# Cross attention's scores in three one-pass fp32r products instead of one fp32 product

## The chip, the core and the metric

The kernel runs on one core of a Trainium2 chip. The metric is the device time of one execution in microseconds; lower is better. The kernel before takes 1884.87 us, the median of 3 runs (1883.82 to 1886.38). The chip's engines run beside each other, each through its own list in order, and wait for each other by semaphores: TensorE (PE, with its weight loads shown as PEld), VectorE (DVE), ScalarE (ACT), GpSimd (POOL) and SyncE (SP), which here issues most DMAs.

## The reference

Two layers of a decoder trunk on 512 tokens of width 1024, batch 1, all in float32. Each layer is a mixer (forgetting attention and a gated recurrence in layer 0, a spatial gating mixer in layer 1), then cross attention into 256 memory tokens, then a mixture of 32 experts. The change is in cross attention, which both layers have:

```python
def memory_cross_attention(xn, memn, wq, wkv, wo, q_gain, k_gain):
    B, S, _ = xn.shape
    q = rms_norm((xn @ wq).reshape(B, S, X_HEADS, X_HEAD_DIM), q_gain)
    k, v = jnp.split(memn @ wkv, 2, axis=-1)
    k = rms_norm(k.reshape(B, MEM_LEN, X_HEADS, X_HEAD_DIM), k_gain)
    v = v.reshape(B, MEM_LEN, X_HEADS, X_HEAD_DIM)
    s = jnp.einsum('bqhd,bkhd->bhqk', q, k, preferred_element_type=jnp.float32) * X_HEAD_DIM ** -0.5
    p = jax.nn.softmax(s, axis=-1).astype(v.dtype)
    o = jnp.einsum('bhqk,bkhd->bqhd', p, v).reshape(B, S, D_MODEL)
    return o @ wo
```

There are 4 heads of 256 channels, so a head's channels fill two blocks of 128 partitions; the whole width is eight blocks, j = 0 to 7, and head h has blocks 2h and 2h + 1.

## The kernel before

Everything is written out by hand: each engine has its own program, and the order of its instructions is the order of the code. Numbers in brackets after L are lines of the kernel.

The large projections are done in float32 by splitting. ScalarE rounds a weight tile of 128 x 512 to fp32r (wh, L575), VectorE computes what is left over (wl, L589 with the norm's gain, L586 without), and TensorE adds three one-pass products: high by high, low by high, high by low (L718, in the helper `dense`). One weight tile is a step. The buffers hold three steps, so a step's wl must be there before TensorE begins the step, and can't be written earlier than three steps ahead. Other work is woven between steps: a `between` table gives for a step's number what an engine does before that step.

Cross attention of a layer runs so:

1. The memory's projection to keys and most of the values (kv 0 to 2), then the queries' projection (xq 0 and 1). Between steps 4 and 6 of xq 0 TensorE turns the normalised keys (L1032); VectorE copies them out of PSUM with their gain to xkT (`k_out`, L2214).
2. The last part of the values' projection (kv 3). Between its steps TensorE turns the first four blocks of the normalised queries xqn (`turn`, L1048), ScalarE copies them with their gain to xqT (`turned`, L1648, signal q_out), and VectorE sums squares and scales the second half of xqn (L1912).
3. The softmax loop over 16 items; an item n is a head and 128 queries. For each n, TensorE does the scores of item n + 3 (`scores`, L1058), turns the probabilities of item n (`transposes`, L1067), after items 1, 3, 5, 7 the next query block (`turn` 4 to 7), and after items 4, 8, 12 the value products of a whole head (`values`, L1077). VectorE takes the maximum of a row of scores (L2230), and per item a reciprocal and the scaling of the probabilities (L2235, L2236); ScalarE does the exponential (L1667), the copy of the turned probabilities (L1675), xqT (L1648) and the high part of a head's output (L1681), whose low part is VectorE's `output_lo` (L2241).
4. The output projection (xo), then the routing and the experts.

Scores need a query block in xqT and the keys in xkT; three PSUM banks hold scores, so item n's scores wait until the exponential of item n - 3 has read its bank (p_done). Query blocks are turned in two PSUM banks, 2 and 3, so `turn(j)` waits until block j - 2 has been copied out.

SyncE issues the loads of the weights in one fixed order. Twelve buffers take expert weights; six are the ring that dense weights use too, others lie over tiles that the earlier stages use, slot7 over `nat` (memory tokens) and slot8 over `gain`. `free_slot` holds what a load waits for.

Of the kernel before, what the change touches and what calls it, by code (L numbers as in the profile page):

```python
# [18 lines left out]
F32 = mybir.dt.float32  # L19
# [7 lines left out]
P = 128  # L27
# [183 lines left out]
def program(nc, A, out):  # L211
    ctx = ExitStack()
    with ctx:
# [73 lines left out]
        def sm(name):  # L287
# [65 lines left out]
        xkn = sb("xkn", [P, MM, D], over="extra", skip=24 * E)  # L353
        xkT = sb("xkT", [P, KD, MEM], over="extra", skip=32 * E)
        xv = sb("xv", [P, MM, D], over="extra", skip=40 * E)
        xqT = sb("xqT", [P, KD, T], over="extra", skip=48 * E)
        xqn = sb("xqn", [P, TM, D], over="extra", skip=16 * E)
# [74 lines left out]
            "rg_sqrt rec_ready rec_hi rec_lo gate_ready "  # L432
            "rows_clear c_rows fs_done fe_done fo_done fo_copied fo_ready fo_hi fo_lo q_turned q_out s_done mx_done p_done pn_done pt_done pt_copied o_done o_hi o_copied "
            "gains_loaded gains_loaded2 gains_turned gains_ready f_scaled k_rounded k_copied gb_scaled u_scaled u_out blocks_loaded mem_loaded spatial_done v_pre v_out vbias_loaded bs_loaded v_scaled ws_loaded ws_masked ws_turned wsT_ready gt_ready gt_hi gt_lo "
# [186 lines left out]
        def _(sp):  # L621
            def free_slot(unit, l):
# [10 lines left out]
                elif SLOT[unit] == RING + 1:  # L633
                    sp.wait_ge(acc_done, PLAIN["nmem", l, MM - 1] + 1)
                    sp.wait_ge(squares, nats_upto("mem", l))
                elif SLOT[unit] == RING + 2:
                    sp.wait_ge(S["rec_ready"], 4)
                elif SLOT[unit] == RING + 3:
                    sp.wait_ge(S["pt_done"], N_ITEMS * (l + 1))
                elif SLOT[unit] == RING + 4:  # L640
                    sp.wait_ge(S["o_done"], X_HEADS * (l + 1))
                elif SLOT[unit] in (RING + 5, ONCE):
                    sp.wait_ge(acc_done, PLAIN["route", l, 0] + 1)
# [50 lines left out]
        def _(pe):  # L694
# [324 lines left out]
            def cross(l):  # L1019
# [22 lines left out]
                def turn(j):  # L1042

                    pe.wait_ge(heads_ready, n0 + 3 + j // 4)
                    if j >= 2:
                        pe.wait_ge(S["q_out"], q0 + (j - 1 if j < 4 else j))
                    for m in range(TM):
# [3 lines left out]
                def scores(n):  # L1051
                    h, i = items_x[n]
                    if i == 0:
                        pe.wait_ge(S["q_out"], q0 + max(2 * h + 2, 4))
                    if n >= SCORES:
                        pe.wait_ge(S["p_done"], t0 + n - SCORES + 1)
                    for kk in range(2):
                        mm = pe.matmul(ps[:, SCORE_BANK[n % SCORES], 0:MEM], xqT[:, 2 * h + kk, i * P:(i + 1) * P],  # L1058
                                       xkT[:, 2 * h + kk, :], start=(kk == 0), stop=(kk == 1))
                    mm.then_inc(S["s_done"], 1)  # L1060
# [789 lines left out]
        def _(dve):  # L1850
# [346 lines left out]
            def cross(l):  # L2197
# [12 lines left out]
                def k_out(r):  # L2210
                    def run():
                        b = round_done(dve, ("xkT", l, r))
                        for j in range(4):
                            ins = dve.tensor_scalar(xkT[:, 4 * r + j, :], ps[:, b + j, 0:MEM], xkg[:, l, j % 2:j % 2 + 1],  # L2214
                                                    None, ALU.mult)
                        ins.then_inc(took(("xkT", l, r)), 1)
                    return run
# [5 lines left out]
                means = lambda *ms: lambda: head_means(("xq", l, 1), ms, 2, X_DIM)  # L2223
                split(("kv", l), 3, {3: means(0, 1), 4: means(2, 3), 7: xqh(1)})
                split_next()
                t0, h0 = N_ITEMS * l, X_HEADS * l

# [22 lines left out]
                for n in range(N_ITEMS):  # L2250
                    normalise(n)
                    if n + SCORES < N_ITEMS:
                        maxima(n + SCORES)
                    if n % TM >= 2 and n > TM:
                        output_lo(n // TM - 1, n % TM - 2)
# [496 lines left out]
```

## Time and profile before

| | |
|---|---|
| median of 3 runs | 1884.87 us |
| profiled execution | 1886.64 us, span 1884.9 us |
| mean granted TensorE clock | 0.996 |
| PE busy | 1848.6 us, 98% |
| DVE busy | 860.6 us, 46% |
| ACT busy | 558.2 us, 30% |
| scores of cross attention (L1058), PE | 32.9 us busy, 128 records of 128x256 |

The span is the time from the first to the last instruction of one profiled execution. A matmul's record is longer than the time it holds TensorE, since the next one starts before it ends: what matters in a row of equal matmuls is the distance between starts. An fp32 product shows as two records, an fp32r product as one; an fp32 turn shows as one. Rows that read "x4" join four neighbouring records of the same form. TensorE's records write f32 for both.

### The profile page before, as it was taken

The page shows a single profiled execution, that of the slowest core. Times are in us where ns is not written, and L with a number is a line of the kernel's source. Part 1 is how long each engine was busy: PE and PEld are TensorE (multiplying, and loading weights), DVE is VectorE, ACT ScalarE, POOL GpSimd, SP SyncE. Part 2 cuts the span into 40 slices and gives each one's busy share as a digit, 9 for nine tenths or more (in the row PEclk, how much of TensorE's full clock was granted, in tenths as well). Part 3 has the DMA queues.
Part 4 walks back from the last instruction along what each step waited for, and adds up shares of the span by engine and source line. Part 5 has one row for each costly group of instructions (what it writes and reads, how often), then busy time and mean ns, then how long its engine had stood idle before and what let it go on. Part 6 is the DMA issues. An engine that isn't in the chain of part 4 may idle for free.

```text
span 1884.9 us, 22147 instructions
## 1 busy us (share of the span) xinstructions
PE 1848.6 (98%) x9054; PEld 1168.7 (62%) x9054; DVE 860.6 (46%) x1384; ACT 558.2 (30%) x1015; POOL 101.1 (5%) x144
## 2 busy tenths in 40 slices
PE   8999999999999999999899999999999999999997
PEld 7775778686454444543588888787784444544543
DVE  4566564546342433433433455455363433433433
ACT  4436353633111111111344433445351111111110
POOL 2200010001000000000000022000010000000000
PEclk9999999999999999999999999999999999999999
DMA  6220243137999999999633321332159999999997
GB/s 238 90 67 23 90 139 107 46 104 306 399 421 421 421 421 420 421 421 421 231 125 116 106 88 69 112 134 90 49 201 370 421 421 422 421 420 421 421 421 298
DMA packets 95640, 486.92 MB, mean 258 GB/s; under 512 B 7776, under 2 KB 7888, under 8 KB 46256
## 3 DMA queue, kind: packets, MB, share of 16 engines
q1 hardware_dynamic: 93408, 479.23, 63.8%
q0 software_dynamic: 1456, 5.14, 0.9%
q8 instruction: 76, 1.25, 0.3%
q10 hardware_dynamic: 672, 1.07, 0.2%
q14 instruction: 28, 0.23, 0.0%
HBM read 483.31 MB, written 2.10 MB: 258 GB/s over the span
## 4 chain that ended last, share of the span: by engine, by line
PE 92%; DMA 3%; DVE 3%; ACT 2%; issue 0%; POOL 0%; SPq 0%; DVEq 0%; POOLq 0%; ACTq 0%
PE ps L718 27%; PE ps L1161 22%; PE ps L1185 11%; PE ps L715 7%; PE ps L1126 6%; PE ps L1147 5%; PE ps L1077 1%; DMA slot<-in_moe_w_down 1%; DMA ring<-in_c_w_in 1%; PE ps L945 1%; PE ps L1058 1%; PE ps L768 1%; PE ps L1221 1%; PE ps L1006 1%; DVE wl L589 1%; PE ps L742 1%
## 5 line engine op out<-in xcount | busy, mean ns | idle before, releaser
L1161 PE MATMUL ps<-ring,xg 128*64 128x512 f32 x1536 | 441.0, 594 | 5.2 <-DMA slot<-in_moe_w_up 2.6
L1161 PEld LDWEIGHTS ps<-ring,xg 128*64 128x64 f32 x1536 | 138.7, 137 | 222.8 <-issue 222.6
L589 DVE SCALAR_TENSOR_TENSOR wl<-ring,gcols,wh 128x512 fp32r<-128x512 f32 x200 | 149.0, 751 | 204.1 <-ACT wh L575 202.7
L1161 PE MATMUL ps<-slot,xg 128*64 128x512 f32 x512 | 224.5, 595 | 0.0
L1185 PE MATMUL ps<-slot,hT 128*64 128x512 f32 x976 | 219.9, 595 | 2.0 <-ACT hT L1741 2.0
L718 PE MATMUL ps<-wh,ah 128*128 128x512 f32 x544 | 216.1, 397 | 5.4 <-DVE wl L589 3.1
L718 PE MATMUL ps<-wh,al 128*128 128x512 f32 x544 | 212.1, 390 | 0.0
L718 PE MATMUL ps<-wl,ah 128*128 128x512 f32 x544 | 211.9, 390 | 0.0
L2412 DVE SCALAR_TENSOR_TENSOR hh<-ps,columns_of,sg 128x512 f32<-128x512 f32 x32 | 36.2, 1130 | 384.7 <-PE ps L1161 384.7
L575 ACT ACTIVATE wh<-ring,gcols 128x512 fp32r<-128x512 f32 x200 | 142.2, 719 | 205.7 <-PE ps L718 161.1
L2433 DVE TENSOR_TENSOR x<-ps,x 128x1024 f32<-128x1024 f32 x120 | 144.2, 1222 | 83.8 <-PE ps L1147 80.0
L1185 PEld LDWEIGHTS ps<-slot,hT 128*64 128x64 f32 x976 | 79.6, 137 | 127.1 <-issue 112.7
L1768 ACT ACTIVATE xg<-ps,grow 128x224 f32<-128x224 f32 (+1 forms) x128 | 50.7, 451 | 267.1 <-PE ps L1126 248.5
L718 PEld LDWEIGHTS ps<-wh,ah 128*128 128x128 f32 x544 | 102.2, 188 | 30.7 <-DVE wl L589 4.8
L718 PEld LDWEIGHTS ps<-wh,al 128*128 128x128 f32 x544 | 102.1, 188 | 21.6
L718 PEld LDWEIGHTS ps<-wl,ah 128*128 128x128 f32 x544 | 102.3, 188 | 20.4 <-issue 0.5
L1126 PEld LDWEIGHTS ps<-oh,xnh 128*128 128x128 f32 x448 | 85.5, 191 | 45.4 <-issue 45.4
L1126 PE MATMUL ps<-oh,xnh 128*128 128x224 f32 (+1 forms) x448 | 109.0, 287 | 0.0
L1161 PEld LDWEIGHTS ps<-slot,xg 128*64 128x64 f32 x512 | 65.4, 137 | 67.3 <-issue 67.3
L1126 PE MATMUL ps<-oh,xnl 128*128 128x224 f32 (+1 forms) x448 | 103.6, 275 | 0.0
L1747 ACT ACTIVATE yh<-ps 128x512 fp32r<-128x512 f32 x64 | 34.8, 594 | 231.8 <-PE ps L1185 223.6
L586 DVE TENSOR_TENSOR wl<-ring,wh 128x512 fp32r<-128x512 f32 x80 | 55.0, 690 | 97.1 <-ACT wh L575 96.9
(338 smaller groups left out, 2678.4 us busy)
## 6 DMA issues: line engine op xcount, KB each, us to landing
slot<-in_moe_w_down SPq DMA_DIRECT2D x126, 1024.0 KB, 14.5
ring<-in_moe_w_gate SPq DMA_DIRECT2D x98, 1024.0 KB, 12.7
ring<-in_moe_w_up SPq DMA_DIRECT2D x94, 1024.0 KB, 15.1
slot<-in_moe_w_up SPq DMA_DIRECT2D x34, 1024.0 KB, 16.6
slot<-in_moe_w_gate SPq DMA_DIRECT2D x30, 1024.0 KB, 12.8
ring<-in_x_wkv SPq DMA_DIRECT2D x16, 1024.0 KB, 5.0
ring<-in_c_w_in SPq DMA_DIRECT2D x16, 1024.0 KB, 5.3
ring<-in_ab_w_in SPq DMA_DIRECT2D x10, 1024.0 KB, 9.7
```

Source lines behind the costliest of these rows:

```text
L575: act.activation(wh[:, t % STAGE, :], ring[:, SLOT[unit], 512 * s:512 * (s + 1)], ACT.Copy, **({} if g is None else dict(scale=g))).then_i ...
L586: dve.tensor_tensor(wl[:, t % STAGE, :], ring[:, SLOT[unit], 512 * s:512 * (s + 1)], wh[:, t % STAGE, :].bitcast(F32), ALU.subtract).then_ ...
L589: dve.scalar_tensor_tensor(out=wl[:, t % STAGE, :], in0=ring[:, SLOT[unit], 512 * s:512 * (s + 1)], scalar=g, in1=wh[:, t % STAGE, :].bitc ...
L715: mm = pe.matmul(ps[:, b + m, 0:T], w[:, (t0 + k) % STAGE, m * P:(m + 1) * P], a[:, k, :], **flags)
L718: mm = pe.matmul(ps[:, b + m, :], a[:, (k + k0) % steps, m * P:(m + 1) * P], w[:, (t0 + k) % STAGE, :], **flags)
L1126: mm = pe.matmul(by_expert(ps[:, bank, kk * 256:(kk + 1) * 256], n), a[:, m, k * P:(k + 1) * P], by_expert(oh[:, b % 2, m, :], n), start=( ...
L1147: mm = pe.matmul(ps[:, bank + half, :], selT[:, q % 2, m * P:(m + 1) * P], a[:, 512 * half:512 * (half + 1)], start=(i == 0), stop=(i == 1))
L1161: mm = pe.matmul(ps[p * SLOTS:(p + 1) * SLOTS, bank, :], xg[:, b % 2, k, r * P + p * SLOTS:r * P + (p + 1) * SLOTS], w(p)[:, k % 4, :], st ...
L1185: mm = pe.matmul(ps[p * SLOTS:(p + 1) * SLOTS, Y + half, :], hT[:, k, p * SLOTS:(p + 1) * SLOTS], w(p)[:, k % 2, 512 * half:512 * (half + 1)],
L1768: ins = act.activation(by_expert(xg[:, b % 2, k, :], n), by_expert(ps[:, bank, kk * 256:(kk + 1) * 256], n), ACT.Copy, scale=grow[:, l, k: ...
L2412: return dve.scalar_tensor_tensor(out=hh[:, :].rearrange("p (k c) -> p k c", k=KF), in0=by_row(ps[:, UP, :]), scalar=wcol[:, 0:1], in1=by_ ...
L2433: return dve.tensor_tensor(x[:, m, :], ps[:, bank:bank + 2, :].rearrange("p a n -> p (a n)"), x[:, m, :], ALU.add)
```

## The change

xkT and xqT become fp32r tiles, that is the rounded high parts. Two tiles hold what rounding took off: xkl for the keys (laid over `nat`) and xql for the queries (laid over `gain`, four blocks at a time). VectorE computes both from the same PSUM banks as the high parts, with the gain: xkl within `k_out`, after waiting for its own writes of xkT (`link`), and xql in the new `query_low(j)`. It waits for ScalarE's xqT block (q_out) and signals q_low; TensorE's `turn` and `scores` now wait for q_low where they waited for q_out. The score of an item is made of three fp32r products for each of its two blocks. SyncE's loads into slot7 and slot8 wait for all scores as well.

```diff
-        xkT = sb("xkT", [P, KD, MEM], over="extra", skip=32 * E)
+        xkT = sb("xkT", [P, KD, MEM], F32R, over="extra", skip=32 * E)
+        xkl = sb("xkl", [P, KD, MEM], F32R, over="nat")
-        xqT = sb("xqT", [P, KD, T], over="extra", skip=48 * E)
+        xqT = sb("xqT", [P, KD, T], F32R, over="extra", skip=48 * E)
+        xql = sb("xql", [P, KD // 2, T], F32R, over="gain")
...
                 elif SLOT[unit] == RING + 1:
                     sp.wait_ge(acc_done, PLAIN["nmem", l, MM - 1] + 1)
                     sp.wait_ge(squares, nats_upto("mem", l))
+                    sp.wait_ge(S["s_done"], N_ITEMS * (l + 1))
                 elif SLOT[unit] == RING + 2:
                     sp.wait_ge(S["rec_ready"], 4)
+                    sp.wait_ge(S["s_done"], N_ITEMS * (l + 1))
...
                     if j >= 2:
-                        pe.wait_ge(S["q_out"], q0 + (j - 1 if j < 4 else j))
+                        pe.wait_ge(S["q_low"], q0 + (j - 1 if j < 4 else j))
...
                     if i == 0:
-                        pe.wait_ge(S["q_out"], q0 + max(2 * h + 2, 4))
+                        pe.wait_ge(S["q_low"], q0 + max(2 * h + 2, 4))
...
                     for kk in range(2):
-                        mm = pe.matmul(ps[:, SCORE_BANK[n % SCORES], 0:MEM], xqT[:, 2 * h + kk, i * P:(i + 1) * P],
-                                       xkT[:, 2 * h + kk, :], start=(kk == 0), stop=(kk == 1))
+                        j = 2 * h + kk
+                        for t, (q_, k_) in enumerate(((xqT[:, j, :], xkT), (xqT[:, j, :], xkl), (xql[:, j % 4, :], xkT))):
+                            mm = pe.matmul(ps[:, SCORE_BANK[n % SCORES], 0:MEM], q_[:, i * P:(i + 1) * P], k_[:, j, :],
+                                           start=(j % 2 == 0 and t == 0), stop=(j % 2 == 1 and t == 2))
...
                             ins = dve.tensor_scalar(xkT[:, 4 * r + j, :], ps[:, b + j, 0:MEM], xkg[:, l, j % 2:j % 2 + 1],
                                                     None, ALU.mult)
+                        link(ins)
+                        for j in range(4):
+                            ins = dve.scalar_tensor_tensor(out=xkl[:, 4 * r + j, :], in0=ps[:, b + j, 0:MEM],
+                                                           scalar=xkg[:, l, j % 2:j % 2 + 1],
+                                                           in1=xkT[:, 4 * r + j, :].bitcast(F32), op0=ALU.mult, op1=ALU.subtract)
...
-                split(("kv", l), 3, {3: means(0, 1), 4: means(2, 3), 7: xqh(1)})
+                def query_low(j):
+                    dve.wait_ge(S["q_out"], q0 + j + 1)
+                    if j >= 4:
+                        dve.wait_ge(S["s_done"], t0 + 2 * TM * (j // 4 - 1) + TM * ((j - 4) // 2 + 1))
+                    dve.scalar_tensor_tensor(out=xql[:, j % 4, :], in0=ps[:, Q_BANK[j], :], scalar=xqg[:, l, j % 2:j % 2 + 1],
+                                             in1=xqT[:, j, :].bitcast(F32), op0=ALU.mult, op1=ALU.subtract)\
+                       .then_inc(S["q_low"], 1)
+
+                def first_lows():
+                    query_low(0)
+                    query_low(1)
+
+                def next_lows():
+                    query_low(2)
+                    query_low(3)
+                    xqh(1)()
+
+                split(("kv", l), 3, {3: means(0, 1), 4: means(2, 3), 6: first_lows, 7: next_lows})
...
                     if n + SCORES < N_ITEMS:
                         maxima(n + SCORES)
+                    if n % 2 and n < 8:
+                        query_low(4 + n // 2)
```

What stands in the engines' lists at the places that matter. First VectorE at the end of the last values' projection (kv 3), before; wl are the weight splits, xqn the scaled queries:

```order
L1903 ISA [waits sq_used]
L589 SCALAR_TENSOR_TENSOR wl<-ring,gcols,wh 128x512 [waits wh_ready] x3
L1912 TENSOR_TENSOR xqn<-ps,rstd 128x512 [waits rstd_ready]
L1912 TENSOR_TENSOR xqn<-ps,rstd 128x512 x3
L1919 ISA [waits taken1]
L589 SCALAR_TENSOR_TENSOR wl<-ring,gcols,wh 128x512 [waits wh_ready]
```

The same place on VectorE, of the change:

```order
L1909 ISA [waits sq_used]
L591 SCALAR_TENSOR_TENSOR wl<-ring,gcols,wh 128x512 [waits wh_ready] x2
L2241 SCALAR_TENSOR_TENSOR xql<-ps,small,xqT 128x512 [waits q_out] x2
L591 SCALAR_TENSOR_TENSOR wl<-ring,gcols,wh 128x512 [waits wh_ready]
L2241 SCALAR_TENSOR_TENSOR xql<-ps,small,xqT 128x512 [waits q_out] x2
L1918 TENSOR_TENSOR xqn<-ps,rstd 128x512 [waits rstd_ready]
L1918 TENSOR_TENSOR xqn<-ps,rstd 128x512 x3
L1925 ISA [waits taken1]
L591 SCALAR_TENSOR_TENSOR wl<-ring,gcols,wh 128x512 [waits wh_ready]
```

Two low parts stand ahead of the split for step 6, two more ahead of the scaling of xqn and the split for step 7. Next VectorE in the softmax loop, items 1 and 2, before (the maximum is that of item n + 3):

```order
L2235 RECIPROCAL rinv<-rsum 128x1 [waits p_done]
L2236 TENSOR_SCALAR prob<-prob,rinv 128x256 [waits dve_chain]
L2230 TENSOR_REDUCE nmax<-ps 128x1 [waits s_done]
L2235 RECIPROCAL rinv<-rsum 128x1 [waits p_done]
L2236 TENSOR_SCALAR prob<-prob,rinv 128x256 [waits dve_chain]
```

The same items on VectorE, of the change:

```order
L2264 RECIPROCAL rinv<-rsum 128x1 [waits p_done]
L2265 TENSOR_SCALAR prob<-prob,rinv 128x256 [waits dve_chain]
L2259 TENSOR_REDUCE nmax<-ps 128x1 [waits s_done]
L2241 SCALAR_TENSOR_TENSOR xql<-ps,small,xqT 128x512 [waits s_done,q_out]
L2264 RECIPROCAL rinv<-rsum 128x1 [waits p_done]
L2265 TENSOR_SCALAR prob<-prob,rinv 128x256 [waits dve_chain]
```

The low part of block 4 stands between item 1's maximum and item 2's reciprocal; blocks 5, 6 and 7 follow in the same way after items 3, 5 and 7. Last TensorE at item 1, before:

```order
L1067 MATMUL ps<-ident,prob 128x128 [waits pn_done]
L1067 MATMUL ps<-ident,prob 128x128
L1048 MATMUL ps<-ident,xqn 128x128 [waits q_out,heads_ready]
L1048 MATMUL ps<-ident,xqn 128x128 x3
L1058 MATMUL ps<-xkT,xqT 128x256 [waits p_done]
L1058 MATMUL ps<-xkT,xqT 128x256
L1067 MATMUL ps<-ident,prob 128x128 [waits pt_copied,pn_done]
```

TensorE at item 1, of the change:

```order
L1073 MATMUL ps<-ident,prob 128x128 [waits pn_done]
L1073 MATMUL ps<-ident,prob 128x128
L1052 MATMUL ps<-ident,xqn 128x128 [waits q_low,heads_ready]
L1052 MATMUL ps<-ident,xqn 128x128 x3
L1064 MATMUL ps<-xkT,xqT 128x256 [waits p_done]
L1064 MATMUL ps<-xkl,xqT 128x256
L1064 MATMUL ps<-xkT,xql 128x256
L1064 MATMUL ps<-xkT,xqT 128x256
L1064 MATMUL ps<-xkl,xqT 128x256
L1064 MATMUL ps<-xkT,xql 128x256
L1073 MATMUL ps<-ident,prob 128x128 [waits pt_copied,pn_done]
```

Two instructions of an item have become six; the turned probabilities behind them still wait for VectorE's scaled ones (pn_done).

## Rows read from the trace of the kernel before

**Rows 1.** The page, part 1: busy time, share of the span, instructions.
```profile
PE 1848.6 (98%) x9054; PEld 1168.7 (62%) x9054; DVE 860.6 (46%) x1384; ACT 558.2 (30%) x1015; POOL 101.1 (5%) x144
```

**Rows 2.** Table by stage, both softmax stretches: busy us, clock, DMA.
```profile
core 0: us, PE busy (x) PEld busy (x) DVE busy (x) ACT busy (x) POOL busy (x), PEclk, DMA share, GB/s
344.00:376.40 32.40, 30.66 (x137) 20.38 (x135) 16.10 (x52) 18.48 (x56) 0.00 (x0) 1.00 0.08 30
1306.40:1338.90 32.50, 30.55 (x136) 20.32 (x134) 15.91 (x52) 19.76 (x58) 0.00 (x0) 1.00 0.08 29
```

**Rows 3.** Chain of waits in order of time: start, us, what.
```profile
353.53 0.87 PE ps L1058 x4
354.40 0.22 PE ps L1067 x2
354.61 3.44 PE ps L1077 x8
```

**Rows 4.** Order of time, TensorE, the experts' gather: start, us, instruction.
```profile
464.98 0.28 PE L1126 MATMUL ps<-oh,xnh 128*128 128x256 f32 x1
...
466.39 0.28 PE L1126 MATMUL ps<-oh,xnh 128*128 128x256 f32 x1
```

**Rows 5.** Order of time, VectorE, first step of the keys.
```profile
297.73 1.66 DVE L2214 TENSOR_SCALAR xkT<-ps,small 128x256 f32<-128x256 f32 x4 [2.62 <-PE ps L1032]
299.31 0.74 DVE L589 SCALAR_TENSOR_TENSOR wl<-ring,gcols,wh 128x512 fp32r<-128x512 f32 x1
```

**Rows 6.** Chain of waits, TensorE around the second turn of keys.
```profile
303.17 0.87 PE ps L1032 x8
304.04 28.65 PE ps L718 x126
```

**Rows 7.** Order of time, end of the last values' projection.
```profile
337.59 0.75 DVE L589 SCALAR_TENSOR_TENSOR wl<-ring,gcols,wh 128x512 fp32r<-128x512 f32 x1 [0.92 <-ACT wh L575]
...
338.56 0.75 DVE L589 SCALAR_TENSOR_TENSOR wl<-ring,gcols,wh 128x512 fp32r<-128x512 f32 x1 [0.23 <-ACT wh L575]
...
339.00 1.03 PE L1048 MATMUL ps<-ident,xqn 128*128 128x128 f32 x8
339.23 2.48 DVE L1912 TENSOR_TENSOR xqn<-ps,rstd 128x512 f32<-128x512 f32 x4
...
341.75 0.75 DVE L589 SCALAR_TENSOR_TENSOR wl<-ring,gcols,wh 128x512 fp32r<-128x512 f32 x1
...
342.56 0.19 PEld L718 LDWEIGHTS ps<-wh,mh 128*128 128x128 f32 x1 [0.15 <-DVE wl L589]
```

**Rows 8.** Groups by line, VectorE: count | busy us, mean ns | idle before.
```profile
L2412 DVE SCALAR_TENSOR_TENSOR hh<-ps,columns_of,sg 128x512 f32<-128x512 f32 x32 | 36.2, 1130 | 384.7 <-PE ps L1161 384.7
...
L2122 DVE SCALAR_TENSOR_TENSOR gt<-ps,norms,vbias 128x512 f32<-128x512 f32 x16 | 11.9, 745 | 0.0
...
L2241 DVE TENSOR_TENSOR al<-ps,ah 128x512 fp32r<-128x512 f32 x16 | 10.8, 685 | 17.9 <-ACT ah L1681 17.9
```

**Rows 9.** Order of time, softmax loop, items 1 to 3.
```profile
350.21 0.60 PE L1048 MATMUL ps<-ident,xqn 128*128 128x128 f32 x4
...
350.85 0.69 ACT L1648 ACTIVATE xqT<-ps,small 128x512 f32<-128x512 f32 x1
...
351.52 0.38 PE L1067 MATMUL ps<-ident,prob 128*128 128x128 f32 x2
...
352.06 0.15 DVE L2235 RECIPROCAL rinv<-rsum 128x1 f32<-128x1 f32 x1
...
352.66 0.44 PE L1067 MATMUL ps<-ident,prob 128*128 128x128 f32 x2
```

**Rows 10.** Order of time, SyncE's queue: the loads into slot6 and slot8.
```profile
425.70 0.80 SPq L666 DMA_DIRECT2D slot<-in_moe_w_up  x2
```

**Rows 11.** Table by stage, columns as in Rows 2.
```profile
894.00:897.00 3.00, 1.86 (x10) 0.46 (x6) 0.00 (x0) 0.00 (x0) 0.00 (x0) 1.00 1.01 421
912.00:915.00 3.00, 1.50 (x6) 1.24 (x7) 2.71 (x6) 0.76 (x2) 0.00 (x0) 0.98 1.05 387
915.00:918.00 3.00, 3.00 (x8) 2.30 (x7) 1.56 (x3) 0.00 (x0) 0.00 (x0) 0.50 1.06 388
```

More of the change, by code:

```diff
@@ L432, in program @@
             "rg_sqrt rec_ready rec_hi rec_lo gate_ready "
-            "rows_clear c_rows fs_done fe_done fo_done fo_copied fo_ready fo_hi fo_lo q_turned q_out s_done mx_done p_done pn_done pt_done pt_copied o_done o_hi o_copied "
+            "rows_clear c_rows fs_done fe_done fo_done fo_copied fo_ready fo_hi fo_lo q_turned q_out q_low s_done mx_done p_done pn_done pt_done pt_copied o_done o_hi o_copied "
             "gains_loaded gains_loaded2 gains_turned gains_ready f_scaled k_rounded k_copied gb_scaled u_scaled u_out blocks_loaded mem_loaded spatial_done v_pre v_out vbias_loaded bs_loaded v_scaled ws_loaded ws_masked ws_turned wsT_ready gt_ready gt_hi gt_lo "
@@ L2223, in cross @@
                 means = lambda *ms: lambda: head_means(("xq", l, 1), ms, 2, X_DIM)
-                split(("kv", l), 3, {3: means(0, 1), 4: means(2, 3), 7: xqh(1)})
+                t0, h0, q0 = N_ITEMS * l, X_HEADS * l, KD * l
+                def query_low(j):
[13 more added lines that the diff above has]
+                split(("kv", l), 3, {3: means(0, 1), 4: means(2, 3), 6: first_lows, 7: next_lows})
                 split_next()
-                t0, h0 = N_ITEMS * l, X_HEADS * l
                 def maxima(n):
```

## The prediction, made before the changed kernel ran

> **What bounds the kernel now.** I read the page first. TensorE is busy for 98% of the span and VectorE for less than half of it [rows 1], which looks as if any cut of TensorE work were a gain. But the change touches one place, the softmax stretch of cross attention, once per layer. So the table by stage comes next: that stretch takes 32.4 us in layer 0 and 32.5 in layer 1; TensorE is busy for about 95% of it, VectorE for half, ScalarE for 57 to 61% [rows 2]. The chain of waits shows TensorE's work back to back there: 0.87 us of scores for one item (a head and 128 queries), 0.22 of turned probabilities, 3.44 of the value products of a head [rows 3]. Last the order of time, since half-idle engines say nothing of a wait in a chain.
>
> **The scores themselves.** An item is two fp32 products of 256 columns. The 0.87 us are four records, 0.2175 each. The new item is six one-pass products. The trace has that form in the experts' gather: fp32r, 128 weights, 256 columns, with a new weight load before each; from 464.98 to 466.39 twelve of them go by, 0.1175 each [rows 4]. Six are 0.705. So an item gains 0.165 to 0.17 us, and 32 items 5.4 us, if nothing else held TensorE. That is all that the change can give.
>
> On this step the Trainium skill ("TensorE: Matmul & The Clock Gate", Part 3 on row and column tiling) says that weight loads overlap running matmuls only where their row groups differ. All six products use the whole array, and by that page's load time of 128/1.2 = 107 ns in front of each 107 ns product an item would take 1.28 us, an estimate that makes the scores 13 us slower over the kernel. The trace disagrees: 0.1175 from product to product with a load for each [rows 4] leaves no room for it.
>
> **Keys.** Each of two xkT steps in a layer gets four more VectorE instructions of 256 columns and a wait for its own last write. The four old ones take 1.66 us together, and the weight split behind them ends at 300.05 [rows 5]; I take 1.75 for the new four, which makes it 301.8. TensorE wants that split at 304.04, after the turn of the second half of the keys [rows 6]: hidden. The second step begins with the end of that turn, so its split would be ready at 304.04 + 1.66 + 1.75 + 0.74 = 308.2, and TensorE wants it two steps of 12 products later; 28.65/126 = 0.227 each [rows 6] put that at 309.5. Hidden too, with 1.3 us to spare. Bounds: 0, and 1.5 a layer if each instruction took twice that.
>
> **Queries, first four parts.** The old order on VectorE at the end of the projection of the last values: splits at 337.59 and 338.56, scaling of xqn 339.23 to 341.7, the last split at 341.75, for which TensorE waits already (0.15 us idle at 342.56) [rows 7]. So this piece of VectorE's queue is on the path. The new order puts query_low(0), (1) before the second of these splits and query_low(2), (3) before the scaling. The price of one query_low: a scalar_tensor_tensor of 512 columns from PSUM takes 0.745 with the operands laid out as here, a plain subtraction 0.685, and one that reads PSUM with a stride 1.130 [rows 8]. I take 0.745, of which about 0.69 pass before the next queued instruction starts; 0.685 and 1.130 are kept as ends. Step by step:
> (a) lows 0 and 1: 338.28 to 339.72. The split for step 6 ends at 340.4 (wanted after 341.3: free).
> (b) TensorE's turn(2) now waits for low(0), turn(3) for low(1): the second turn runs 339.80 to 340.24 instead of ending at 339.80. ScalarE hands out q_out(3) at 341.17.
> (c) low(2) from 340.44, low(3) from 341.17 to 341.86; the scaling and its signal take 2.52 as before (339.23 to 341.75); the last split starts at 344.38 instead of 341.75.
> Everything behind it is late by 2.63 us. TensorE, done with step 6 at 343.0, stands for some 2.1. Ends: 1.5 (if ScalarE and VectorE overlap better than I lay them out) and 4.1 (1.130 for each low).
>
> **Queries, last four parts.** In the softmax loop query_low(4 to 7) comes after the maximum of items 1, 3, 5, 7, and the reciprocal and scaling of the next item are queued behind it. It waits for a chain: turn on TensorE, xqT on ScalarE. From [rows 9], counted from the turn's start at 350.21: ScalarE starts at +0.64 (350.85), is done at +1.33, low starts at +1.36, the next reciprocal at +2.06, and from a reciprocal to the turned probabilities it is 0.60 (352.06 to 352.66). So transposes(2) starts at +2.66; before, at +1.31 (351.52). TensorE has only the scores of one item in between and stands for 1.5 us. Pair by pair, with the 0.17 of each item that is on the path and the idle time that TensorE had already:
> - before the first turn: -0.17
> - turn 4 to transposes 3: +1.35 - 0.17 - 0.05 = +1.13
> - turn 5 to transposes 5: +1.36 - 0.17 = +1.19
> - turn 6 to transposes 7: +1.35, and 0.34 back, since VectorE had a late output_lo in this place already: +1.01
> - turn 7 to transposes 8: output_lo (0.60) now stands in the queue behind the low: +1.95
> - items 9 to 15: two items' worth back, -0.34; the rest is hidden behind VectorE's chain of maximum, scaling and output_lo.
> Sum +4.77 a layer. Ends: +4.4 with the plain subtraction's price, +6.4 with 1.130 each.
>
> **The added waits on the DMA queue.** Two prefetches of expert weights now also wait for the last score. They stand in the queue behind a load that waits for the end of the output projection and goes out at 425.70 [rows 10], 50 us after the last score. Cost 0. The rest of the expert phase waits for that same projection, so a delay of the stretch moves it as a whole; I find nothing there to take it up.
>
> **Sum.** 2.63 + 4.77 = 7.4 us a layer, and both layers run the same stretch in the same time [rows 2]: +14.8. The profiled execution took 1886.64 for a span of 1884.9, so it would become 1901.4; it is 1.8 above the median of the runs, and on the median 1884.87 the sum gives 1899.7.
>
> **The rivals.**
> 1. *VectorE's work is hidden, the scores' gain remains.* On averages it would fit: 8 lows at 0.69 are 5.5 us a layer, and VectorE is idle for 16.3 of 32.4 [rows 2]. Then 1884.87 - 5.4 = 1879.5. It decides if a low can start by about 0.6 after its turn, before the next reciprocal is due; the ScalarE step alone ends at +1.33 [rows 9]. Chance 4%.
> 2. *Half of the stalls is hidden*, because engines reorder less strictly than my walk or the handoffs are shorter: about +4 to +10, 1889 to 1895, or, if still more is hidden, no change. 14%.
> 3. *The clock falls.* TensorE would stand 1.5 to 2.2 us four times in 18 us, and once before. In this trace the granted clock went to 0.50 (1.2 of 2.4 GHz) at 915, after a stretch in which TensorE had been busy for 1.50 of 3 us, yet stayed at 1.00 through 894 to 897, busy for 1.86 of 3 [rows 11]. The new stretch with its stalls is nearer to these two than anything in the old one. A fall costs half of what TensorE does meanwhile; the row at 0.50 is 3 us long [rows 11], so 1.5 to 2 us each time. One or two falls a layer: +3 to +7 on top, 1903 to 1907. 17%.
> 4. *One-pass products aren't cheaper at this width.* If each took the 0.2175 of the old records, an item would take 1.30; the four items of a layer that lie in a stall hide it, 24 others would pay 0.6 more than in my sum: 1914. Twelve products in 1.41 us speak against it [rows 4]. 3%. The skill's rule on weight loads would come to the same time.
> The forecast with its own spread, 1895 to 1904: 62%.
>
> **Numbers.** The likeliest case gives 1899.7. The range for 8 in 10 takes in the ends of the lows' price (two layers of 4.1 + 6.4 make 1906) and most of rivals 2 and 3: 1891 to 1907. A difference under 0.2%, 3.8 us, can't be told from none. Faster: rival 1, 4%. Within it: the end of rival 2, 4%. Slower: 92%.
>
> **What would show it.** Scores six to an item, 0.117 apart. Lows near 0.75 us, eight a layer. The wait of TensorE's L718 products for the last split of the projection some 2.1 us; turned probabilities waiting for prob 1.5 us after each of turns 4, 5, 6 and 2.2 after turn 7, and VectorE's lows waiting for ScalarE's xqT. The stretch from the first score to the output projection 37.2 us instead of 32.4. The clock at 1.00 in it. It is wrong if TensorE goes through the turns without a gap, if lows take over 0.9, or if another stage changes its length.

## The result, and the profile after

The changed kernel takes 1899.53 us (median of four runs, 1896.62 to 1900.83), the kernel before 1884.34 beside it (1881.19 to 1886.38). The ratio is 1.0080 (95%: 1.0068 to 1.0092): slower by 15.2 us. The forecast was 1899.7. The profiled execution of the change took 1898.58 us for a span of 1896.8. The page, part 1 (busy time, share of the span, instructions), answers to [rows 1]:

```profile
PE 1847.4 (97%) x9118; PEld 1170.2 (62%) x9118; DVE 877.3 (46%) x1416; ACT 559.5 (29%) x1015; POOL 101.2 (5%) x144
```

TensorE does slightly less work than before (1847.4 us against 1848.6) in a span that is 12 us longer. So the 12 us are standing time, and the shares do not say where. The table by stage does. The two stretches from the first score to the output projection of the change, columns as in [rows 2] (stretch, length, busy us of PE, PEld, DVE, ACT, POOL, clock, DMA share, GB/s):

```profile
346.82:383.92 37.10, 28.97 (x168) 21.00 (x166) 18.36 (x55) 18.78 (x56) 0.00 (x0) 1.00 0.06 25
1311.85:1350.93 39.08, 31.26 (x167) 22.14 (x166) 18.40 (x55) 20.07 (x57) 0.00 (x0) 0.94 0.04 17
```

In layer 0 the stretch takes 37.10 us where it took 32.32 (344.07 to 376.39, from the exact starts; [rows 2] rounds them), and TensorE is busy for 28.97 of it. Layer 1 has the same and 2 us more, with a clock of 0.94, of which below.

The scores in order of time (start, us, instruction; a record's 0.28 us contains time that overlaps its neighbours):

```profile
346.82 0.28 PE L1064 MATMUL ps<-xkT,xqT 128*128 128x256 f32 x1
346.93 0.28 PE L1064 MATMUL ps<-xkl,xqT 128*128 128x256 f32 x1
347.05 0.28 PE L1064 MATMUL ps<-xkT,xql 128*128 128x256 f32 x1
...
347.40 0.28 PE L1064 MATMUL ps<-xkT,xql 128*128 128x256 f32 x1
```

From the first to the sixth 0.58 us, 0.116 from one to the next, as in the gather [rows 4]. The scores did become cheaper, as the change intended. The loss is in the chain of waits. Its steps around the turn of query block 4 (start, us, engine, what), against the back-to-back TensorE work of [rows 3]:

```profile
352.96 0.45 PE ps L1052 x4
353.41 0.02 issue
353.44 0.70 ACT xqT L1654
354.13 0.02 issue
354.16 0.75 DVE xql L2241
354.91 0.08 DVE rinv L2264
354.99 0.02 issue
355.01 0.36 DVE prob L2265
355.38 0.04 issue
355.42 0.44 PE ps L1073 x2
355.86 0.71 PE ps L1064 x6
```

It goes TensorE, ScalarE, VectorE and back: turn, high part, low part, reciprocal, scaling, turned probabilities, and then the scores of the next item, 0.71 us for six products. A piece of the chain starts where the one before it ends; by the order of time the turn itself starts at 352.80. The turned probabilities start at 355.42, 2.62 us later, where it was 1.31 before [rows 9]. In these 2.62 us TensorE has the turn and the scores of one item, about half of the time. In order of time, this turn and TensorE's turned probabilities after the four turns (in brackets the idle time ahead of them and what ended it):

```profile
352.80 0.60 PE L1052 MATMUL ps<-ident,xqn 128*128 128x128 f32 x4
...
355.42 0.44 PE L1073 MATMUL ps<-ident,prob 128*128 128x128 f32 x2 [1.33 <-DVE prob L2265]
...
359.25 0.44 PE L1073 MATMUL ps<-ident,prob 128*128 128x128 f32 x2 [1.32 <-DVE prob L2265]
...
366.50 0.44 PE L1073 MATMUL ps<-ident,prob 128*128 128x128 f32 x2 [1.33 <-DVE prob L2265]
...
371.38 0.44 PE L1073 MATMUL ps<-ident,prob 128*128 128x128 f32 x2 [1.93 <-DVE prob L2265]
```

And the end of the last values' projection, in order of time, against [rows 7]:

```profile
337.72 0.75 DVE L591 SCALAR_TENSOR_TENSOR wl<-ring,gcols,wh 128x512 fp32r<-128x512 f32 x1 [0.92 <-ACT wh L577]
338.39 1.40 DVE L2241 SCALAR_TENSOR_TENSOR xql<-ps,small,xqT 128x512 fp32r<-128x512 f32 x2
...
340.67 1.41 DVE L2241 SCALAR_TENSOR_TENSOR xql<-ps,small,xqT 128x512 fp32r<-128x512 f32 x2 [0.22 <-ACT xqT L1654]
341.99 2.47 DVE L1918 TENSOR_TENSOR xqn<-ps,rstd 128x512 f32<-128x512 f32 x4
344.50 0.75 DVE L591 SCALAR_TENSOR_TENSOR wl<-ring,gcols,wh 128x512 fp32r<-128x512 f32 x1
```

The last weight split starts at 344.50 instead of 341.75. The stage began 0.14 us later in this trace, so 2.61 of that are the low parts'. The waits of this stage and the loop in the change (engine and line, what it waited for, total us, times, longest):

```profile
DVE xql L2241 <- ACT xqT L1654: 4.7, 5, 1.4
...
PEld ps L722 <- DVE wl L591: 2.4, 1, 2.4
PE ps L722 <- DVE wl L591: 1.9, 1, 1.9
```

TensorE stands once for the last split, and VectorE's low parts wait for ScalarE's xqT: VectorE is half idle and still late.

**Where the 11.9 us of this pair of profiled executions are** (1898.58 less 1886.64), by the starts of TensorE's first turn, first score and first output projection in both traces:

| stretch | layer 0, before, after | layer 1, before, after |
|---|---|---|
| first turn to first score | 11.54, 14.15 (+2.61) | 11.55, 15.13 (+3.58) |
| first score to output projection | 32.32, 37.10 (+4.78) | 32.54, 39.08 (+6.54) |
| from there to the next layer's turn, or the end | 918.34, 912.80 (-5.54) | 546.1, 545.9 (-0.2) |

The beginning adds 0.14. Two things in this table were not in the sum. Layer 1 lost 2.7 us more than layer 0, and 5.5 us came back between the layers. The clock has a part in both. In the trace of before it fell at 434, 915 and 1396, in the trace of the change at 1310, 1337 and 1409: three falls each, but two of the change's lie inside layer 1's stretches and two of before's between the layers. The last section has the rest.

### The profile page after: what moved, and what is told of

It reads as the page before. It is cut to its first block, busy times and chain, and to the rows that moved or that the text cites. A ratio compares the mean times of both kernels' runs of the same rounds, so it can differ in the third digit from the quotient of the medians.

```text
span 1896.8 us, 22317 instructions
## 1 busy us (share of the span) xinstructions
PE 1847.4 (97%) x9118; PEld 1170.2 (62%) x9118; DVE 877.3 (46%) x1416; ACT 559.5 (29%) x1015; POOL 101.2 (5%) x144
## 3 DMA queue, kind: packets, MB, share of 16 engines
q10 hardware_dynamic: 672, 1.07, 0.2%
## 4 chain that ended last, share of the span: by engine, by line
PE 90%; DMA 4%; DVE 4%; ACT 2%; issue 0%; POOL 0%; SPq 0%; DVEq 0%; POOLq 0%; ACTq 0%
PE ps L722 27%; PE ps L1167 22%; PE ps L1191 11%; PE ps L719 7%; PE ps L1132 6%; PE ps L1153 5%; PE ps L1083 2%; DMA slot<-in_moe_w_up 1%; DMA ring<-in_c_w_in 1%; DMA ring<-in_moe_w_gate 1%; PE ps L949 1%; PE ps L772 1%; PE ps L1227 1%; DVE wl L591 1%; PE ps L1010 1%; PE ps L746 1%
## 6 DMA issues: line engine op xcount, KB each, us to landing
slot<-in_moe_w_down SPq DMA_DIRECT2D x126, 1024.0 KB, 14.6
ring<-in_moe_w_gate SPq DMA_DIRECT2D x98, 1024.0 KB, 12.9
ring<-in_moe_w_up SPq DMA_DIRECT2D x94, 1024.0 KB, 15.3
```

## The experiments

Three jobs, each on one chip with its own runs of the kernel before (medians 1883.32, 1883.25 and 1883.5). The lengths "per layer" below are those of the table above, first turn to first score and first score to output projection, layer 0 then layer 1; before has 11.54, 32.32 and 11.55, 32.54. A star marks a stretch in which a fall of the clock began; after the first stall the fall reaches 1 to 3 us into the loop as well.

### The scores alone

All six products of an item use the high parts, so the low parts' terms are missing from the scores; nothing computes a low part, and no wait is added.

```diff
-for t, (q_, k_) in enumerate(((xqT[:, j, :], xkT), (xqT[:, j, :], xkl), (xql[:, j % 4, :], xkT))):
+for t, (q_, k_) in enumerate(((xqT[:, j, :], xkT), (xqT[:, j, :], xkT), (xqT[:, j, :], xkT))):
```

> The six one-pass products per item stay, but all of them use the rounded high parts: no low parts are computed and the waits are the old ones (q_out, no wait of the DMA queue). Theory (VectorE's chain of maximum, reciprocal, scaling sets the end of many items): only part of the 5.4 us comes through; walked with the durations of the trace of before, the softmax stretch loses 1.15 us a layer, so 2.3 us in all, ratio to before 0.9988, and the stretch from first score to output projection goes from 32.4 to about 31.2. Rival (TensorE alone sets the end): 2.7 us a layer, 5.4 in all, ratio 0.9971, stretch 29.7. Turned probabilities wait for prob more often than before by the theory, not by the rival.

Measured: 1878.23 us, ratio 0.9973 (0.9961 to 0.9986). Per layer 11.54, 31.27 and 11.56, 31.47: the softmax stretch is shorter by 1.05 and 1.07, not by 2.7. The waits of its stretch, TensorE's for VectorE (total us, times, longest):

```profile
PEld ps L1071 <- DVE prob L2258: 2.8, 6, 1.0
PE ps L1071 <- DVE prob L2258: 1.4, 3, 0.8
```

The matmuls' own idle time for prob was 0.9 us in the trace of before, and it is 1.4 now. So of the 2.7 us a layer that cheaper scores take from TensorE's work, 1.06 reach the end; the rest turns into idle time of TensorE. That VectorE's chain sets the pace in those items is what the forecast's walk says; the longer wait for prob agrees with it. The walk's number for the stretch (1.15) stands. The total does not: -5.1 us against -2.1 from the stretches. The difference lies outside them (last section).

> The same kernel as fast_scores_only (all six products use the high parts, no low parts computed). Its two stretches were 1.05 us shorter each, 2.1 in all, while its time was 5.1 us lower. If the rest was chance, the ratio now lies at or above 0.9980, and falls of the clock show in its trace; if the kernel itself gains outside the stretches, the ratio stays at 0.9973 and the part between the stretches, 916.3 us then, 918.3 before, is short again.

On another chip 1879.87, ratio 0.9979 (0.9970 to 0.9988); per layer 11.53, 31.27 and 11.55, 31.49. The stretches repeat to 0.02 us; -3.6 in the total again exceeds their -2.1.

### The keys' low parts and the added waits on the DMA queue, with the old scores

```diff
+                        link(ins)
+                        for j in range(4):
+                            ins = dve.scalar_tensor_tensor(out=xkl[:, 4 * r + j, :], ...)
...
+                    sp.wait_ge(S["s_done"], N_ITEMS * (l + 1))
```

> The kernel before with the keys' low parts computed as well (not used by the scores) and the two added waits of the DMA queue. Theory: both hidden, 0 us, ratio 1.000; no wait of TensorE for wl at the keys' steps. Rival: the eight instructions show, up to 1.5 us a layer, ratio 1.0016; or the DMA waits delay the first expert weights and the first products of the experts wait for slot loads.

Measured: 1883.4, ratio 1.0000 (0.9991 to 1.0009), both pairs of stretches as before. The new work is there and is hidden; VectorE at the first step of the keys, in order of time:

```profile
297.78 1.66 DVE L2217 TENSOR_SCALAR xkT<-ps,small 128x256 f32<-128x256 f32 x4 [2.58 <-PE ps L1035]
299.48 1.66 DVE L2221 SCALAR_TENSOR_TENSOR xkl<-ps,small,xkT 128x256 fp32r<-128x256 f32 x4
301.05 1.41 DVE L590 SCALAR_TENSOR_TENSOR wl<-ring,gcols,wh 128x512 fp32r<-128x512 f32 x2
```

Four key lows take 1.66 us, and behind them the splits run at once, ahead of TensorE's demand at 304.04 [rows 6]. SyncE's load goes out at 425.74, against 425.70 in [rows 10]. Both terms of 0 hold. This trace shows only the first step of the keys; for the second, the unchanged ratio speaks.

### The first four low parts moved

`query_low(0)`, `(1)` follow step 5's split, `(2)`, `(3)` come behind the last split; all else as in the change.

```diff
-                split(("kv", l), 3, {3: means(0, 1), 4: means(2, 3), 6: first_lows, 7: next_lows})
+                split(("kv", l), 3, {3: means(0, 1), 4: means(2, 3), 5: first_lows, 7: xqh(1)})
+                query_low(2)
+                query_low(3)
```

> The changed kernel with the first four low parts elsewhere in VectorE's list: 0 and 1 one step earlier, 2 and 3 behind the last weight split instead of ahead of the scaling. Theory: the stall of 2.1 to 2.6 us a layer at the end of the last values' projection goes, 0.2 us of it stay; 4.8 us less than the changed kernel, about 10 more than before, ratio to before 1.0054. Rival (the stall is only a symptom and TensorE would wait at the first scores instead, for q_low): no change against the changed kernel, ratio 1.008.

Measured: 1891.79, ratio 1.0050 (1.0036 to 1.0064). Per layer 11.55, 37.11 and 11.55, 37.33: the first stall is gone to 0.01 us, the loop's remains whole. The two waits in its trace (total us, times, longest):

```profile
PEld ps L1073 <- DVE prob L2267: 8.7, 9, 2.1
...
PEld ps L722 <- DVE wl L591: 0.2, 1, 0.2
```

The wait for the last weight split was 2.4 us in the trace of the change and is 0.2.

### The loop's low parts one item later

```diff
-                    if n % 2 and n < 8:
-                        query_low(4 + n // 2)
+                    if n % 2 == 0 and 0 < n <= 8:
+                        query_low(3 + n // 2)
```

The low part of block 4 now follows item 2's maximum, behind item 2's reciprocal and scaling. TensorE's order, and every wait on it, is that of the change.

> The changed kernel with the low parts of blocks 4 to 7 one item later in VectorE's list (after the maximum of iterations 2, 4, 6, 8), when ScalarE's xqT is long there. Theory (the place of the instruction costs, not its duration): the loop loses all but 0.1 us of its 4.77 a layer; 9.4 us less than the changed kernel, about 5.4 more than before, ratio to before 1.0029. VectorE's low parts no longer wait for xqT. Rival (VectorE's added work costs, wherever it stands: four of 0.69 a layer): the loop keeps 2.8 us a layer, ratio to before 1.0058.

Measured: 1888.15, ratio 1.0022 (1.0013 to 1.0032). Per layer 15.08*, 32.43 and 14.14, 32.59: the loop is back at 0.11 and 0.05 us above before, the first stall remains. So the 4.8 us a layer came from the place of four instructions in VectorE's list, not from the dependence itself or from their duration. VectorE's wait for ScalarE's xqT in this trace, all of it among the first four low parts, is

```profile
DVE xql L2241 <- ACT xqT L1654: 0.2, 1, 0.2
```

where in the change it was 4.7 us in five waits.

### Both moved

> Both moves together, the whole computation intact. Theory: 0.2 us a layer left at the projection and 0.1 in the loop, 0.6 us above before, ratio 1.0003, not to be told from before; the gain of the faster scores is used up by VectorE's four added instructions in the loop. The stretch from first score to output projection takes 32.5 us. Rival (the two stalls hide each other's cost): a ratio of 1.002 or more.

Measured: 1880.53, ratio 0.9987 (0.9978 to 0.9996). Per layer 11.55, 32.38 and 11.54, 32.58, within 0.06 of before, with a low part for every block. The table by stage of its two stretches:

```profile
344.15:376.53 32.38, 28.37 (x167) 21.00 (x166) 19.23 (x57) 18.34 (x56) 0.00 (x0) 1.00 0.07 30
1300.49:1333.07 32.58, 28.35 (x168) 20.97 (x166) 19.26 (x57) 19.62 (x57) 0.00 (x0) 1.00 0.07 29
```

TensorE is busy for 28.4 of the 32.4 us, where it was for 30.7 [rows 2]. Most of the scores' saving is there, but as idle time. With the cheap scores and without low parts the same loop took 31.27, so the low parts and their waits still cost 1.1 us a layer, which is what the cheap scores brought. The two moves together are worth 18.9 us to the change (1899.43 on this chip, below). Each alone is compared by its distance from before on its own chip, since the medians of before differ by 1 us: the change is 15.2 above, first_lows_moved 8.5 and loop_lows_later 4.8, so the moves bring 6.7 and 10.4.

> The same kernel as both_moved. Its stretches were those of before within 0.1 us, its time 2.4 us lower, with no fall of the clock in its trace. If that was chance, ratio 0.999 to 1.001 and at least one fall in the trace; if it is the kernel's, 0.9987 again and none.

On another chip 1881.1, ratio 0.9990 (0.9981 to 0.9999); per layer 11.55, 32.38 and 11.54, 32.59.

### The low parts with the old scores

The change with the two fp32 products of before in `scores` and unrounded xqT and xkT; the low parts are computed in their places and not used.

> The changed kernel's low parts, waits and order, but the scores as before: two fp32 products per item, low parts unused. Theory: the stalls hide half of the scores, so giving up the fast products costs only 0.85 us a layer, 1.7 in all: about 16.9 us above before, ratio 1.0090. Rival (scores count in full): 2.7 a layer, 20.6 us above before, ratio 1.0109.

Measured: 1899.77, ratio 1.0087 (1.0073 to 1.0101). Per layer 14.70*, 37.94 and 14.89*, 38.16. The stretch is 0.84 us longer than the change's in layer 0 (37.10). In layer 1 it is 0.80 over the repetition of the change (37.36, with the end of a fall in its first part) and 0.83 over first_lows_moved (37.33, no fall). The forecast's pair-by-pair terms give -0.17 in the five places that they name, 0.85. This says what the cheap scores earn inside the changed kernel: 0.8 us of 2.7 a layer. The totals are too coarse to show it: on this chip the change has 1899.43, 0.3 us less, where the two stretches give 1.7.

### The stalls filled

Five idle products go to TensorE ahead of the scores behind each turn, into the bank that these will overwrite; what they compute is discarded. The kernel has the helper already.

```diff
                     pe.wait_ge(S["p_done"], ...)
+                    if n in (5, 7, 9, 11):
+                        idle_products(SCORE_BANK[n % SCORES], 5)
```

> The changed kernel, with five one-pass products of 512 columns (1.1 us) ahead of the scores of items 5, 7, 9 and 11, into the score bank that these scores then overwrite: TensorE works through most of the loop's four stalls per layer. If the granted clock costs nothing, the time is that of the changed kernel, ratio to before 1.008 (0.3 us a layer more at most). If falls of the clock in the loop are part of its time, the clock stays at 1.00 through the loop in both layers and the time is 1.5 to 3 us lower than the changed kernel's, ratio 1.0065.

Measured: 1895.64, ratio 1.0062 (1.0049 to 1.0076), 3.8 us under the change on the same chip. Per layer 14.68*, 37.18 and 14.27*, 37.39. The table by stage of its loops:

```profile
347.19:384.37 37.18, 34.52 (x187) 25.58 (x186) 18.48 (x55) 18.75 (x56) 0.00 (x0) 0.97 0.06 23
...
1315.70:1353.07 37.37, 34.99 (x187) 25.99 (x186) 18.58 (x55) 20.14 (x57) 0.00 (x0) 0.96 0.06 25
```

TensorE is busy for 34.5 and 35.0 us, where the change has 29.0 in layer 0, and the length of the stretch is within 0.1 of a stretch of the change without a fall: the stalls are waits for the chain, whatever TensorE does in them. The clock shows below 1.00 here because the fall after the first stall reaches into the stretch's beginning; no fall began within either loop. But the loops of first_lows_moved and of lows_with_old_scores, without filler, had none either, so two loops do not show that the filler prevents it. So it is not shown that the filler is worth the 3.8 us; they are more than the stretches give.

### The change again

> The changed kernel on the same chip, for the comparison with those above: ratio 1.008. Its trace tells whether the clock falls in layer 1 at the same places again (1309 to 1314 and 1336 to 1341) or anywhere else; by theory the falls differ from run to run, while the stalls don't.

Measured: 1899.43, ratio 1.0080 (1.0067 to 1.0094). Per layer 14.15, 38.79* and 14.45*, 37.36. The fall is in layer 0's loop this time, in layer 1's before. Two of the four loops of this kernel are at 37.1 and 37.4 us, two at 38.8 and 39.1.

### The turns spread

From both moved, the turns (and ScalarE's copies) go from items 1, 3, 5, 7 to 0, 3, 6, 7, and the low parts follow items 1, 4, 7 and 8.

```diff
-                    if n % 2 and n < 8:
-                        turn(4 + n // 2)
+                    if n in (0, 3, 6, 7):
+                        turn(4 + (0, 3, 6, 7).index(n))
```

> both_moved with the turns of blocks 4 to 7 after items 0, 3, 6 and 7 instead of 1, 3, 5 and 7, and their low parts one item later each, so that two of them stand beside value products. Walked with the durations of before the loop takes 0.4 us a layer less than before's, 31.9 instead of 32.3: 0.8 us in all, ratio to both_moved 0.9996, too small for the runs, but not for the trace. Rival (VectorE is no longer the limit anywhere in the loop): nothing changes, 32.4.

Measured: 1880.02, ratio 0.9985 (0.9976 to 0.9994). Per layer 11.55, 32.08 and 11.54, 32.27: 0.30 and 0.32 less than both_moved_again on the same chip, 0.24 and 0.27 less than before, where 0.4 was expected. The totals of the two versions, 1880.02 and 1881.1, can't be told apart.

> The kernel before, as a kernel of its own: ratio 1.000. Its trace adds a second sample of where the granted clock falls. If falls come by chance, at the routing (435, 1395) and at the end of layer 0's experts (915), one at each place or none, their number differs from the 3 of the first trace, and with it the length of what lies outside the softmax stretches; the stretches stay 32.3 and 32.5 us.

Measured: 1883.31, ratio 1.0000 (0.9991 to 1.0009); per layer 11.54, 32.31 and 11.55, 32.54.

## Why the prediction was right

Step by step, by its own terms.

**The scores.** Forecast 0.705 for an item from a gather row; it is 0.71 in the chain. With a weight load for each, products stand 0.116 apart. The rule on row groups that the Trainium skill gives ("TensorE: Matmul & The Clock Gate", Part 3), taken by itself, would have made the item 1.28 us by the prediction's estimate; the measurement decides against it. The term was not only priced but placed: the gain counts only in items where TensorE is the last. The scores alone and the old scores in the change measured this from both sides, 1.06 a layer (the walk: 1.15) and 0.80 to 0.84 (the walk: 0.85), of the 2.7 that a sum of durations would promise.

**Keys and DMA waits.** Forecast 0 and 0; measured 1.0000 and unchanged stretches.

**The first four low parts.** Forecast 2.63; 2.61 in layer 0 of the trace, 2.59 in the one layer 1 without a fall (loop_lows_later), and the move takes them back to 0.01. The price was 0.745 for one; the tile's group in the trace of the change (count, then ns min/median/max, first and last start) says

```profile
L2241 DVE SCALAR_TENSOR_TENSOR xql<-ps,small,xqT x16: 740/750/751, 338.4 to 1334.8; 128x512 fp32r<-128x512 f32 x16
```

TensorE's wait was forecast as "some 2.1"; it is 2.4 for its weight load and 1.9 for the matmul.

**The last four.** Forecast 4.77 a layer; 4.78 in layer 0, where no fall came, and 4.79 in layer 1 of first_lows_moved. The terms hold one by one as well, by the starts in layer 0 of both traces: before the first turn -0.16 (forecast -0.17), then +1.17, +1.22, +0.96 and +1.92 for turns 4 to 7 (forecast 1.13, 1.19, 1.01, 1.95), and -0.27 from there to the output projection (forecast -0.34). The stalls themselves were forecast at 1.5, 1.5, 1.5 and 2.2 us and show as 1.33, 1.32, 1.33 and 1.93. Each wait is 0.2 to 0.3 shorter than forecast, the delay is not: the sum was made from differences between starts, and the end of a matmul in a record is modelled. After turn 7 the output_lo queued behind the low part did what the walk said, in order of time in the chain:

```profile
369.52 0.75 DVE xql L2241
370.27 0.60 DVE al L2270
370.87 0.08 DVE rinv L2264
...
370.98 0.36 DVE prob L2265
...
371.38 0.44 PE ps L1073 x2
371.82 3.44 PE ps L1083 x8
```

Low part, output_lo, reciprocal, scaling, all ahead of TensorE's next step.

**The rivals.** Rivals 1, 2 and 4 are out: the stalls were not hidden, and one-pass products were not dearer. Rival 1 was wrong on both halves, since even without low parts only 2.1 of the 5.4 us would have come through. It also set all eight low parts against VectorE's idle time in the loop, though only four stand there. Rival 3, the clock, was set as an alternative with 17%. It came true and yet the forecast held; the sign "the clock at 1.00 in it" failed in two of four loops. The table by stage of layer 1 in the trace of the change, and of layer 0 in its repetition, around the wait after turn 7:

```profile
1335.00:1338.00 3.00, 1.30 (x4) 0.78 (x5) 2.37 (x7) 1.04 (x5) 0.00 (x0) 0.83 0.00 0
1338.00:1341.00 3.00, 3.00 (x6) 1.22 (x5) 0.00 (x0) 0.06 (x1) 0.00 (x0) 0.60 0.00 0
```

```profile
368.00:371.00 3.00, 1.48 (x12) 1.27 (x12) 1.61 (x5) 1.85 (x6) 0.00 (x0) 1.00 0.02 5
371.00:374.00 3.00, 2.60 (x5) 1.15 (x6) 1.10 (x4) 0.84 (x3) 0.00 (x0) 0.64 0.00 0
374.00:377.00 3.00, 3.00 (x8) 1.44 (x7) 0.00 (x0) 0.00 (x0) 0.00 (x0) 0.79 0.00 0
```

Behind 3 us with TensorE busy for 1.3 and 1.5 the granted clock of the next 3 us is 0.60 and 0.64: for most of them the lower of its two levels, 1.2 GHz. The eight value products there take 5.08 and 5.13 us instead of 3.44; in the chain of the first of the two traces

```profile
1337.19 5.08 PE ps L1083 x8
```

That is 1.7 us a fall, where 1.5 to 2 was forecast. A fall behind the first stall costs less, 0.1 to 1.0 us (14.27 to 15.13 where 14.14 and 14.15 stand without one). Together the falls in the stretches cost 2.7 us in this trace and 2.0 in its repetition. This was about offset by 1.3 us and perhaps more gained outside the stretches, which the forecast did not have (last section). So the mechanism was right, and both halves of the sum were right to 0.02 us, while the agreement of the total to 0.2 us is partly luck: +14.8 in the stretches without falls, falls on top, a gain elsewhere against them. On the second chip the change was 16.2 above before, not 15.2. The order of the two halves shows in the totals as well: moving the first lows brought 6.7 us, moving the loop's 10.4, against 5.2 and 9.4 in the stretches. The surplus of 1.0 to 1.5 us is within what the intervals leave open.

## What to carry to other kernels

An instruction in an in-order queue costs what is queued behind it, not its duration: four low parts of 0.75 us cost 4.8 us because each waited for an engine that had just been asked, ahead of work that TensorE needed; the same four one item later cost 0.1. Before trusting "VectorE is busy for half of the time" as cover, follow the chain from the trigger to the reader in starts from the trace, and put a late consumer behind the urgent work in the queue. And a cut of TensorE's work is worth only the share of it that lies where TensorE ends the wait (here 0.4 of it without the stalls). The version with both moved and the one with the turns spread are 1% below the change and about 0.1% below before (0.9987, 0.9990 and 0.9985). For both moved the stretches explain none of this last 0.1%, for the turns spread 0.5 us of it.

## What the runs showed of the hardware that was not expected

**After the same stall the clock falls in some executions and not in others.** In the traces with the first stall (the change twice, loop_lows_later, lows_with_old_scores, stalls_filled) it fell after it in 7 of 10 layers, after the same wait. In the nine traces without this stall, 18 layers, it never did, nor in their loops. In the long loops with unfilled stalls it fell in 2 of the 4 of the changed kernel and in none of the 4 of first_lows_moved and lows_with_old_scores. What decides between two equal stretches no run here shows. Outside these stretches falls come at 434 to 442, 910 to 932 and 1390 to 1413, in the traces of before as well: none to three in a trace, apart from one at the very end of each. By the 1.7 us above a single profiled execution carries up to 5 us of this, an estimate.

**1.3 us at the end of layer 0's experts.** The chain waits there for the first weights of the following projection. Their load goes out at the start of the piece, when TensorE has used a buffer of the ring for the last time. The piece in the chain of before, and of the change:

```profile
884.64 25.05 DMA ring<-in_c_w_in
```

```profile
890.71 23.79 DMA ring<-in_c_w_in
```

In the four traces of kernels with two products to an item it lasts 24.98 to 25.25 us, in the ten with six 23.68 to 23.90, whether the kernel is faster or slower than before. For the two runs of both moved, stretches and this piece make +0.1 - 1.3 = -1.2 us where the ratios say -2.4 and -1.9 (each to 1.7); for the scores alone -2.1 - 1.3 = -3.4 where they say -5.1 (to 2.4) and -4.0 (to 1.7). Within the intervals, though all four lie on the same side, so something may be missing still (the next paragraph has a candidate). The two groups differ in the number of TensorE's instructions (9054 records on the page against 9118, or 9158 with the filler). The difference lies in the softmax stretches, of which layer 0's ends 500 us before this place. It goes with the scores and not with VectorE's work: lows_with_old_scores, which has all low parts, is in the first group, and the scores alone, without any, in the second. Why a transfer there should be shorter is not shown.

**The boundary between the layers**, from the landing of that transfer to the first products of the next layer's projection, goes with the same two groups, if less cleanly. In the four traces with two products to an item it lasts 14.45 to 14.50 us, in lows_with_old_scores too, which has no fall near it. In the ten with six it lasts 11.6 us (three traces, no fall near it), 12.9 to 13.1 (four, one fall), 14.6 (the filler, a longer fall) and 15.3 (two, one fall); their mean is 13.2. So the kernels with six products may gain another 1.3 us here on average, about what is missing above. That is read from few traces, and no run was aimed at it. In the pair of the first table the -5.54 us are -1.46 ahead of the transfer, where before has its fall at 434, -1.26 for the transfer, and -2.82 behind it, where before has its fall at 915. How much of the last is the fall stays open, since the 14.5 us come without one as well.
